# Attention on pairs of heads on partition halves, with the probabilities turned by a product with a diagonal and the output made with channels on partitions

## The chip, the cores and the metric

The kernel runs on one core of a Trainium2 chip (trn2), all in f32. The time is the device time of one execution in microseconds. A core has TensorE (PE; its weight loads are shown apart as PEld), VectorE (DVE), ScalarE (ACT), GpSimd (POOL) and SyncE (SP), which issues most DMAs.

## The reference, cut to what matters

Two blocks of two layers each follow one another on 256 tokens of width 1024 (the first block also on 256 context tokens). Three of the four mixers hold a softmax attention with heads of 64 channels; four query heads share a key head:

```python
def _softmax_attend(q, k, v):            # first block, layer 0
    s = jnp.einsum('bhgqd,bhkd->bhgqk', q, k, ...) * (ATT_HEAD_DIM ** -0.5)
    p = jax.nn.softmax(s, axis=-1).astype(v.dtype)
    return jnp.einsum('bhgqk,bhkd->bhgqd', p, v)
```

- First block, layer 0: 8 query heads, 2 key heads. The 256 context tokens see 256 keys, the 256 others see all 512. Its output is joined with that of a gated linear attention (GLA) and multiplied by `even_w_out`.
- Second block, layer 0: 16 query heads, 4 key heads, causal over 256 tokens.
- Second block, layer 1: the same heads, a causal window of 128 tokens, and a learned sink for each head: the maximum is taken over the logits and the sink, and exp(sink - m) is added to the sum.

Behind each of the two comes the product with `w_o`, a layer norm and a feed-forward part or a mixture of experts.

## The kernel before, in words

Tokens stand in tiles of 128 on the partitions; `hT` holds activations turned, channels on partitions, as the stationary operand of the next product. A stage is a function that adds a body for every engine; engines wait for one another by counted semaphores, and each stage ends with `meet()` (line 197), at which the four compute engines wait for one another. Within a stage each engine does its work in the order in which it is written. SyncE streams weights into a ring of three slots ahead of the stage that uses them.

`attend` (line 1034) is called three times: from `first_layer_even` (line 1569, two heads to a unit) and from `second_attention` (line 2451, four heads to a unit). For each key head `kv`:

- GpSimd copies the four query heads of the group into `att_qs` (line 1070), TensorE turns them, each 64 channels wide (line 1121), ScalarE and VectorE copy two heads each into the lower half of `hT` (lines 1165 and 1212). The keys of all key heads have been turned before (line 1079) and copied by ScalarE (line 1138). All turned queries and keys lie on partitions 0 to 63.
- The units of the key head run over tiles of queries and groups of heads: scores (line 1090, 64 rows of the array), on VectorE the mask where there is one (line 1182) and the maximum (lines 1187, 1191), on ScalarE the exponentials with their sums (line 1150), on TensorE the turning of the probabilities with `nc.tensor.transpose` (line 1101), ScalarE's copy of them (line 1160), then the output with the turned probabilities as weights and 64 columns of values moving (line 1110). VectorE divides by the sums as it takes the output, and writes it over the queries in `A` (lines 1203, 1205).
- TensorE's order is scores of unit i, turning of i-1, output of i-2 (lines 1126 to 1132), and it starts anew for each key head: the next queries are turned when all exponentials of the last head are done (line 1118).

The first attention has 16 units (8 with 256 keys, 8 with 512), each of the others 8 units of four heads (4 with 128 keys, 4 with 256).

`turn` (line 244) then turns the outputs with transposes, eight to a tile of tokens (line 256), ScalarE copies them into `hT` (line 263), and `project` (line 470) multiplies (line 504). In the first layer `gla_pairs` (line 791) stands between `attend` and `turn`; it has products on halves of the array's rows (line 854: two heads, partitions 0 to 63 and 64 to 127) and of its columns (line 872).

The expert products use column halves with `tile_position=(0, 64 * j)` (line 2673).

## Time and profile before

| | us |
|---|---|
| median of 3 runs | 3667.36 (3664.38 to 3670.75) |
| profiled execution | 3668.35 |
| its span | 3666.5 |
| mean granted clock of TensorE | 0.917 |

The page calls a stretch of time by its start and end from the span's start. In a timeline row stand the start, the length, the engine and line, the operation, what it writes and reads, its shape and how often it came; "weights rows*columns, then partitions x moving columns" is the shape of a matmul. A matmul of f32 operands appears as two instructions (passes), a transpose as one. The length of a row that joins several matmuls ends with a modelled end of the last; starts are measured. The clock column is the clock granted to TensorE as a share of 2.4 GHz.

### The profile page before, as it was taken

Reading aid. Unit: us, or ns where it says so; the run is one execution under the profiler, and the core shown is the slowest. Engines: PE = TensorE matmul, PEld = TensorE weight load, DVE = VectorE, ACT = ScalarE, POOL = GpSimd, SP = SyncE. Lnnn points to the kernel's source line nnn. Section 1 sums busy time; section 2 is a strip of 40 time slices with the busy share of each in tenths; the row PEclk is TensorE's granted clock in tenths of the full one; section 3 lists DMA queues with packets and bytes.
Section 4 is the critical chain, followed back from the end, with each engine's and each line's share of the span. In section 5 each row is a group of like instructions: output and inputs, shape, how many; then the busy total and the mean of one; then the engine's idle time right before and its main releaser. Section 6 shows DMA issues by size and latency. Waiting matters only on the chain.

```text
span 3666.5 us, 41927 instructions
## 1 busy us (share of the span) xinstructions
PE 3318.7 (91%) x18452; PEld 1955.5 (53%) x18452; DVE 819.8 (22%) x1241; ACT 452.6 (12%) x992; POOL 290.7 (8%) x286
## 2 busy tenths in 40 slices
PE   6959869999998999889988999977799999999996
PEld 2436644444447778756746677555344444434443
DVE  1032671000026656610012100223200000000002
ACT  1013212000012222210012000012000000000001
POOL 1010540000001222310000000000000000000000
PEclk9975878999999999989985999976799999999998
DMA  8750001120212121214330443130798999899982
GB/s 325 263 200 1 1 1 58 69 87 34 103 29 66 47 58 41 92 64 174 133 143 12 172 161 121 58 118 12 278 359 345 373 367 350 345 384 358 347 346 87
DMA packets 204261, 603.00 MB, mean 164 GB/s; under 512 B 5709, under 2 KB 46893, under 8 KB 197425
## 3 DMA queue, kind: packets, MB, share of 16 engines
q1 hardware_dynamic: 199664, 589.45, 42.4%
q0 software_dynamic: 3952, 10.26, 0.9%
q8 instruction: 149, 2.44, 0.3%
q10 hardware_dynamic: 464, 0.60, 0.1%
q14 instruction: 32, 0.25, 0.0%
HBM read 599.24 MB, written 1.05 MB: 164 GB/s over the span
## 4 chain that ended last, share of the span: by engine, by line
PE 85%; DVE 7%; issue 3%; ACT 2%; DMA 2%; POOL 1%; PEld 0%; POOLq 0%; PEldq 0%; ACTq 0%; DVEq 0%; SPq 0%
PE ps_ffn_gate L582 9%; PE ps_ffn_up L582 9%; PE ps_ffn_down L618 9%; PE ps_hg_step L1769 6%; PE ps_moe_down L2718 5%; PE ps_moe_gate L2673 5%; PE ps_moe_up L2673 5%; PE ps_project L504 4%; PE ps_lin L1432 3%; PE ps_moe_gate L2678 3%; PE ps_moe_up L2678 3%; PE ps_moe_down L2724 3%; PE ps_lin L296 2%; PE ps_att_s L1090 2%; PE ps_att_o L1110 2%
## 5 line engine op out<-in xcount | busy, mean ns | idle before, releaser
L582 PE MATMUL ps_ffn_gate<-hT,ring_buf 128*128 128x256 f32 (+1 forms) x1152 | 344.2, 453 | 6.4 <-DVEq L204 4.0
L582 PE MATMUL ps_ffn_up<-hT,ring_buf 128*128 128x256 f32 (+1 forms) x1152 | 336.7, 445 | 1.3
L618 PE MATMUL ps_ffn_down<-ring_buf,ffn_hiddenT 128*128 128x512 f32 x752 | 325.9, 593 | 3.0 <-issue 3.0
L582 PEld LDWEIGHTS ps_ffn_gate<-hT,ring_buf 128*128 128x128 f32 x1152 | 222.5, 194 | 122.6 <-issue 100.9
L582 PEld LDWEIGHTS ps_ffn_up<-hT,ring_buf 128*128 128x128 f32 x1152 | 217.9, 190 | 110.3 <-issue 90.0
L1769 PE MATMUL ps_hg_step<-ring_buf,hT 128*128 128x256 f32 (+1 forms) x1280 | 247.3, 353 | 18.6 <-ACT hg_kT L1872 16.2
L618 PEld LDWEIGHTS ps_ffn_down<-ring_buf,ffn_hiddenT 128*128 128x128 f32 x752 | 141.7, 190 | 182.0 <-issue 181.9
L1769 PEld LDWEIGHTS ps_hg_step<-ring_buf,hT 128*128 128x128 f32 x1280 | 215.0, 204 | 40.3 <-ACT hg_kT L1872 18.3
L662 DVE TENSOR_TENSOR ffn_hiddenT<-ffn_silu_buf,ps_ffn_up 128x256 f32<-128x256 f32 (+1 forms) x72 | 36.2, 502 | 757.8 <-PE ps_ffn_up L582 757.8
L2673 PE MATMUL ps_moe_up<-ring_buf,moe_xg_buf 128*64 128x512 f32 (+1 forms) x1024 | 199.5, 542 | 0.0
L2841 DVE TENSOR_TENSOR moe_hidden_buf<-moe_silu_buf,ps_moe_up 128x768 f32<-128x768 f32 (+1 forms) x32 | 27.3, 854 | 662.8 <-PE ps_moe_up L2678 590.3
L2718 PE MATMUL ps_moe_down<-ring_buf,moe_hiddenT 128*64 128x512 f32 x768 | 170.1, 595 | 0.0
L504 PE MATMUL ps_project<-ring_buf,hT 128*128 128x512 f32 x320 | 145.0, 615 | 2.7 <-ACTq L204 2.7
L2673 PE MATMUL ps_moe_gate<-moe_third,moe_xg_buf 128*64 128x512 f32 (+1 forms) x768 | 142.8, 524 | 0.0
L637 ACT ACTIVATE ffn_silu_buf<-ps_ffn_gate 128x256 f32<-128x256 f32 (+1 forms) x72 | 32.3, 449 | 849.7 <-PE ps_ffn_gate L582 849.7
L1432 PE MATMUL ps_lin<-ring_buf,hT 128*128 128x448 f32 (+1 forms) x384 | 134.1, 503 | 0.0
L2673 PEld LDWEIGHTS ps_moe_up<-ring_buf,moe_xg_buf 128*64 128x64 f32 x1024 | 70.7, 137 | 114.1 <-issue 106.0
L2783 ACT ACTIVATE moe_silu_buf<-ps_moe_gate 128x768 f32<-128x768 f32 (+1 forms) x32 | 23.4, 732 | 726.3 <-PE ps_moe_gate L2678 726.3
L2718 PEld LDWEIGHTS ps_moe_down<-ring_buf,moe_hiddenT 128*64 128x64 f32 x768 | 53.0, 137 | 104.0 <-issue 104.0
L1432 PEld LDWEIGHTS ps_lin<-ring_buf,hT 128*128 128x128 f32 x384 | 72.1, 193 | 66.5 <-issue 62.1
L504 PEld LDWEIGHTS ps_project<-ring_buf,hT 128*128 128x128 f32 x320 | 62.6, 198 | 83.2 <-issue 83.2
L2678 PE MATMUL ps_moe_up<-ring_buf,moe_xg_buf 128*32 128x256 f32 (+1 forms) x2048 | 103.5, 354 | 0.0
(456 smaller groups left out, 3721.0 us busy)
## 6 DMA issues: line engine op xcount, KB each, us to landing
...
moe_third<-in_w_exp_gate_dram SPq DMA_DIRECT2D x8, 2048.0 KB, 10.1
...
```

What stands on the lines that cost most here:

```text
L296: mm = nc.tensor.matmul(ps[n % 4][:, 0:hi - lo], hT[:, k, t * P:(t + 1) * P], view[:, k, o:o + hi - lo], start=k == 0, stop=k == parts - 1)
L504: mm = nc.tensor.matmul(ps_y[i % 2][:, h * 512:(h + 1) * 512], hT[:, k, t * P:(t + 1) * P], view[:, k, :], start=k == 0, stop=k == KD - 1)
L582: mm = nc.tensor.matmul(ps[:, 0:wide], view[:, k, i * P:(i + 1) * P], hT[:, k, first_col:first_col + wide], start=k == 0, stop=k == KD - 1)
L618: mm = nc.tensor.matmul(ps_y[i % 2][:, h, :], hidT[:, b, i * P:(i + 1) * P], view[:, b, h * 512:(h + 1) * 512], start=first, stop=end)
L1090: mm = nc.tensor.matmul(ps_s[i % 2][:, h, 0:nk], qT[:, g + h, qi * P:(qi + 1) * P], kT[:, bass.ds(kv, 1), 0:nk].rearrange("k h n -> k (h n)"),
L1110: mm = nc.tensor.matmul(ps_o[i % 2][:, h * E:(h + 1) * E], probsT[:, i % 2, h, k, :], A[:, t0 + k, bass.ds(kv * E + v_col, E)], start=k == ...
L1432: mm = nc.tensor.matmul(ps_lin[:, n % 4, 0:hi - lo], hT[:, k, t * P:(t + 1) * P], view[:, k, o:o + hi - lo], start=k == 0, stop=k == KD - 1)
L1769: mm = nc.tensor.matmul(ps[:, 0:width], hT[:, k, t * P:(t + 1) * P], view[:, k, 0:width], start=k == 0, stop=k == KD - 1)
L2673: nc.tensor.matmul(ps[j * 64:(j + 1) * 64, 0:half], xg[:, k, 0:WIDE], w[:, k, j * half:(j + 1) * half], start=k == 0, stop=k == KD - 1, ti ...
L2678: mm = nc.tensor.matmul(ps[j * 32:(j + 1) * 32, half:half + quarter], xg[:, k, WIDE:ROOM], w[:, k, j * quarter:(j + 1) * quarter], start=k ...
L2718: nc.tensor.matmul(ps_y[j * 64:(j + 1) * 64, 0:512], x, w[:, b, j * 512:(j + 1) * 512], start=c == 0 and b == 0, stop=c == NP - 1 and b == ...
L2724: mm = nc.tensor.matmul(ps_y[j * 32:(j + 1) * 32, 512:768], x, w[:, b, j * 256:(j + 1) * 256], start=c == 0 and b == 0, stop=c == NP - 1 a ...
```

## The change

(The lines that the diff removes from `attend` are those printed above; below stand the lines that it adds.)

The unit is now a pair of heads, 16 for each of the three calls, in one sequence over all key heads. A pair's turned queries lie on all 128 partitions, head 0 on 0 to 63 and head 1 on 64 to 127; the turned keys stand twice, once on each half, made by a product with the identity on the two column halves of the array. The score products of the two heads so lie on the two row halves. The queries and keys of the next key head are turned between the units of the last one, through one more PSUM bank; GpSimd has no part any more.

VectorE makes, from the sums, the inverse and two diagonal matrices (the identity scaled by the inverse of each row's sum). The probabilities are turned by a product with the diagonal, which divides as well; ScalarE copies head 0 of the result and VectorE head 1. In the output product the values are the weights (64 columns) and the turned probabilities move (128 columns), the two heads on the two column halves: the output comes with channels on partitions. ScalarE copies it to where the next projection reads it: over the queries in `A` in the first layer (where `project` now takes an accessor `of`), into `hT` in the second block. So `turn` handles four blocks instead of eight in the first layer and is gone from the second block. TensorE's order is scores of i, turning of i-2, output of i-3.

```diff
--- before.py
+++ after.py
-    def project(w, tiles, Y, seam):
+    def project(w, tiles, Y, seam, of=lambda k, t: hT[:, k, t * P:(t + 1) * P]):
...
-                            mm = nc.tensor.matmul(ps_y[i % 2][:, h * 512:(h + 1) * 512], hT[:, k, t * P:(t + 1) * P],
-                                                  view[:, k, :], start=k == 0, stop=k == KD - 1)
+                            mm = nc.tensor.matmul(ps_y[i % 2][:, h * 512:(h + 1) * 512], of(k, t), view[:, k, :],
+                                                  start=k == 0, stop=k == KD - 1)
...
+    def attend(A, q_col, k_col, v_col, kv_heads, q_tiles, room_T, made, mask=None, sinks=None, scale=1.0):
+        E = ATT_D
+        t0, nt = q_tiles[0][0], len(q_tiles)
         nkt = max(k for _, ks in q_tiles for k in ks) + 1 - t0
+        units = [(kv, qi, p) for kv in range(kv_heads) for qi in range(nt) for p in range(2)]
+        n, per = len(units), 2 * nt
+        step = 512 // (nt * P)
+        turns = [("k", 0)] + [("q", b) for b in range(0, 2, step)]
+        rounds = [(kv, kind, b) for kv in range(kv_heads) for kind, b in turns]
+        stands = {i: [] for i in range(n)}
+        for r, (kv, kind, b) in enumerate(rounds):
+            stands[0 if kv == 0 else (kv - 1) * per + 1 + r % len(turns)].append(r)
+        taken = lambda kind, r: sum(1 for x in rounds[:r + 1] if x[1] == kind)
+        ready_of = {"q": "att_q_ready", "k": "att_k_ready"}
+        keys_of = lambda u: q_tiles[units[u][1]][1]
         with ExitStack() as cx:
+            qT = hT[:, 0:4, :].rearrange("p k n -> p (k n)").rearrange("p (b n) -> p b n", n=nt * P) if nt == 4 else \
+                hT[:, :, 0:nt * P]
+            kT = sb(cx, "att_kT", [P, kv_heads, nkt * P])
+            probs = sb(cx, "att_probs_buf", [P, 2, 2, nkt * P])
+            diag = sb(cx, "att_diag_buf", [P, 2, 2, P])
+            masked = sb(cx, "att_masked", [P, 2, 2, nkt * P]) if mask is not None else None
+            stat = sb(cx, "att_stat", [P, 4, 4, 2])
+            probsT = room_T(cx, nkt)
+            ps_s = [pb(cx, f"ps_att_s{i}", [P, 2, 512]) for i in range(2)]
+            ps_t = pb(cx, "ps_att_t", [P, 2, 4, P])
+            ps_o = pb(cx, "ps_att_o", [P, 512])
+            ps_q = pb(cx, "ps_att_q", [P, 512])
             S = s_att
...
+                def stage(r):
+                    kv, kind, b = rounds[r]
+                    if r > 0:
+                        before = ready_of[rounds[r - 1][1]]
+                        pe.wait_ge(S[before].handle, S[before].at(taken(rounds[r - 1][1], r - 1)))
+                    if kind == "k":
+                        for i in range(nkt):
+                            for h in range(2):
+                                mm = nc.tensor.matmul(ps_q[h * E:(h + 1) * E, i * P:(i + 1) * P],
+                                                      A[:, t0 + i, k_col + kv * E:k_col + (kv + 1) * E], ident,
+                                                      start=True, stop=True, tile_position=(0, h * E))
+                    else:
+                        for x in range(step):
+                            for i in range(nt):
+                                at = q_col + (2 * kv + b + x) * 2 * E
+                                mm = nc.tensor.transpose(ps_q[:, (x * nt + i) * P:(x * nt + i + 1) * P],
+                                                         A[:, t0 + i, at:at + 2 * E], ident)
+                    mm.then_inc(S["att_staged"].handle, 1)
+                def scores(u):
+                    kv, qi, p = units[u]
+                    nk = len(keys_of(u)) * P
+                    r = max(x for x in range(len(rounds)) if rounds[x][0] == kv)
+                    pe.wait_ge(S["att_q_ready"].handle, S["att_q_ready"].at(taken("q", r)))
+                    pe.wait_ge(S["att_k_ready"].handle, S["att_k_ready"].at(taken("k", r)))
+                    pe.wait_ge(S["att_probs"].handle, S["att_probs"].at(u - 1))
+                    for h in range(2):
+                        mm = nc.tensor.matmul(ps_s[u % 2][:, h, 0:nk], qT[h * E:(h + 1) * E, 2 * kv + p, qi * P:(qi + 1) * P],
+                                              kT[h * E:(h + 1) * E, kv, 0:nk], start=True, stop=True)
+                def turned(u):
+                    pe.wait_ge(S["att_probs"].handle, S["att_probs"].at(u + 1))
+                    pe.wait_ge(S["att_diag"].handle, S["att_diag"].at(u + 1))
+                    pe.wait_ge(S["att_T_ready_a"].handle, S["att_T_ready_a"].at(u))
+                    pe.wait_ge(S["att_T_ready_v"].handle, S["att_T_ready_v"].at(u))
+                    for h in range(2):
+                        for k in range(len(keys_of(u))):
+                            mm = nc.tensor.matmul(ps_t[:, h, k, :], probs[:, u % 2, h, k * P:(k + 1) * P], diag[:, u % 2, h, :],
+                                                  start=True, stop=True)
+                def output(u):
+                    kv, qi, p = units[u]
+                    keys = keys_of(u)
+                    pe.wait_ge(S["att_T_ready_a"].handle, S["att_T_ready_a"].at(u + 1))
+                    pe.wait_ge(S["att_T_ready_v"].handle, S["att_T_ready_v"].at(u + 1))
+                    pe.wait_ge(S["att_taken"].handle, S["att_taken"].at(u))
+                    for k in range(len(keys)):
+                        for h in range(2):
+                            mm = nc.tensor.matmul(ps_o[h * E:(h + 1) * E, 0:P], A[:, t0 + k, v_col + kv * E:v_col + (kv + 1) * E],
+                                                  probsT[:, u % 2, h, k, :], start=k == 0, stop=k == len(keys) - 1,
+                                                  tile_position=(0, h * E))
...
+                for i in range(n + 3):
+                    if i < n:
+                        for r in stands[i]:
+                            stage(r)
+                        scores(i)
+                    if 2 <= i < n + 2:
+                        turned(i - 2)
+                    if i >= 3:
+                        output(i - 3)
...
+                def queries(r):
+                    kv, kind, b = rounds[r]
+                    act.wait_ge(S["att_staged"].handle, S["att_staged"].at(r + 1))
+                    nc.scalar.activation(qT[:, 2 * kv + b:2 * kv + b + step, :],
+                                         ps_q[:, :].rearrange("p (x n) -> p x n", x=step), ACT.Copy, scale=scale)\
+                        .then_inc(S["att_q_ready"].handle, 1)
+                def softmax(u):
+                    nk = len(keys_of(u)) * P
+                    act.wait_ge(S["att_max"].handle, S["att_max"].at(u + 1))
+                    act.wait_ge(S["att_turned"].handle, S["att_turned"].at(u - 1))
+                    src = ps_s[u % 2] if mask is None else masked[:, u % 2, :, :]
+                        nc.scalar.activation(stat[:, u % 4, 3, :], stat[:, u % 4, 3, :], ACT.Exp)
+                    for h in range(2):
+                        last = nc.scalar.activation(probs[:, u % 2, h, 0:nk], src[:, h, 0:nk], ACT.Exp,
+                                                    bias=stat[:, u % 4, 0, h:h + 1], accum_out=stat[:, u % 4, 1, h:h + 1])
+                def take_turned(u):
+                    nk = len(keys_of(u))
+                    act.wait_ge(S["att_turned"].handle, S["att_turned"].at(u + 1))
+                    act.wait_ge(S["att_out"].handle, S["att_out"].at(u - 1))
+                    nc.scalar.activation(probsT[:, u % 2, 0, 0:nk, :], ps_t[:, 0, 0:nk, :], ACT.Copy)\
+                        .then_inc(S["att_T_ready_a"].handle, 1)
+                def take(u):
+                    kv, qi, p = units[u]
+                    act.wait_ge(S["att_out"].handle, S["att_out"].at(u + 1))
+                    nc.scalar.activation(made(2 * kv + p, qi), ps_o[:, 0:P], ACT.Copy).then_inc(S["att_taken"].handle, 1)
+                for i in range(n + 3):
+                    if i < n:
+                        for r in stands[i]:
+                            if rounds[r][1] == "q":
+                                queries(r)
+                    if 2 <= i < n + 2:
+                        take_turned(i - 2)
+                    if i < n:
+                        softmax(i)
+                    if i >= 3:
+                        take(i - 3)
...
+                def keys(r):
+                    kv, kind, b = rounds[r]
+                    dve.wait_ge(S["att_staged"].handle, S["att_staged"].at(r + 1))
+                    nc.vector.tensor_copy(kT[:, kv, :], ps_q[:, 0:nkt * P]).then_inc(S["att_k_ready"].handle, 1)
+                def maxima(u):
+                    kv, qi, p = units[u]
+                    nk = len(keys_of(u)) * P
+                    dve.wait_ge(S["att_scores"].handle, S["att_scores"].at(u + 1))
+                    src = ps_s[u % 2][:, :, 0:nk]
+                    top = stat[:, u % 4, 0, :]
+                        link_v(nc.vector.tensor_tensor(masked[:, u % 2, :, 0:nk], src,
+                                                       mask[:, qi, 0:nk].unsqueeze(1).to_broadcast([P, 2, nk]), ALU.add))
+                        src = masked[:, u % 2, :, 0:nk]
+                        nc.vector.tensor_reduce(top, src, AX.X, ALU.max, negate=True).then_inc(S["att_max"].handle, 1)
+                        own = sinks[:, 4 * kv + 2 * p:4 * kv + 2 * p + 2]
+                        nc.vector.tensor_tensor(stat[:, u % 4, 3, :], top, own, ALU.add)\
+                def take_turned(u):
+                    nk = len(keys_of(u))
+                    dve.wait_ge(S["att_turned"].handle, S["att_turned"].at(u + 1))
+                    dve.wait_ge(S["att_out"].handle, S["att_out"].at(u - 1))
+                    nc.vector.tensor_copy(probsT[:, u % 2, 1, 0:nk, :], ps_t[:, 1, 0:nk, :])\
+                        .then_inc(S["att_T_ready_v"].handle, 1)
+                def diagonal(u):
+                    total, inverse = stat[:, u % 4, 1, :], stat[:, u % 4, 2, :]
+                    dve.wait_ge(S["att_probs"].handle, S["att_probs"].at(u + 1))
+                        link_v(nc.vector.tensor_tensor(total, total, stat[:, u % 4, 3, :], ALU.add))
+                    for h in range(2):
+                        last = nc.vector.tensor_scalar(diag[:, u % 2, h, :], ident, stat[:, u % 4, 2, h:h + 1], None, ALU.mult)
+                    last.then_inc(S["att_diag"].handle, 1)
+                for i in range(n + 2):
+                    if i < n:
+                        for r in stands[i]:
+                            if rounds[r][1] == "k":
+                                keys(r)
+                        maxima(i)
+                    if i >= 2:
+                        take_turned(i - 2)
+                    if i < n:
+                        diagonal(i)
+            for k in ("att_scores", "att_max", "att_probs", "att_diag", "att_turned", "att_T_ready_a", "att_T_ready_v",
+                      "att_out", "att_taken"):
...
+        attended = lambda b, t: A[:, t, O_AQ + b * P:O_AQ + (b + 1) * P]
         silu_columns(A, O_G, O_Z)
         gla_gates(A, g, T, lambda: even_queries_keys(A))
-        attend(A, O_AQ, O_AK, O_AV, 2, [(0, (0, 1)), (1, (0, 1)), (2, (0, 1, 2, 3)), (3, (0, 1, 2, 3))], 2)
+        attend(A, O_AQ, O_AK, O_AV, 2, [(0, (0, 1)), (1, (0, 1)), (2, (0, 1, 2, 3)), (3, (0, 1, 2, 3))],
+               lambda cx, nkt: hT[:, 4:8, :].rearrange("p k n -> p (k n)")
+               .rearrange("p (b h t n) -> p b h t n", b=2, h=2, t=nkt), attended)
         gla_pairs(A, g, T)
-        turn(lambda t, k: A[:, t, O_G + k * P:O_G + (k + 1) * P] if k < 4 else
-             A[:, t, O_AQ + (k - 4) * P:O_AQ + (k - 3) * P], ALL_TILES)
+        turn(lambda t, k: A[:, t, O_G + k * P:O_G + (k + 1) * P], ALL_TILES, 4)
 
...
             rotate_partly(B, rot)
-            attend(B, 0, K2, V2, 4, [(0, (0,)), (1, (0, 1))], 4, mask=mask, sinks=sinks, scale=ATT_D ** -0.5)
-            turn(lambda t, k: B[:, t - 2, k * P:(k + 1) * P], LAT_TILES)
+            attend(B, 0, K2, V2, 4, [(0, (0,)), (1, (0, 1))],
+                   lambda cx, nkt: sb(cx, "att_probsT", [P, 2, 2, nkt, P]),
+                   lambda b, qi: hT[:, b, (2 + qi) * P:(3 + qi) * P], mask=mask, sinks=sinks, scale=ATT_D ** -0.5)
 
...
         with ExitStack() as cy:
-            project(a["even_w_out"][0], ALL_TILES, A[:, :, 0:D], GatedSeam(cy, 0, 0, (0, 1), ALL_TILES))
+            project(a["even_w_out"][0], ALL_TILES, A[:, :, 0:D], GatedSeam(cy, 0, 0, (0, 1), ALL_TILES),
+                    lambda k, t: hT[:, k, t * P:(t + 1) * P] if k < 4 else
+                    A[:, t, O_AQ + (k - 4) * P:O_AQ + (k - 3) * P])
```

## Rows read from the trace of the kernel before

**Rows 1.** The page, part 1: busy time, share, instructions

```profile
PE 3318.7 (91%) x18452; PEld 1955.5 (53%) x18452; DVE 819.8 (22%) x1241; ACT 452.6 (12%) x992; POOL 290.7 (8%) x286
```

**Rows 2.** Stretches: us, busy of PE, PEld, DVE, ACT, POOL, clock, DMA share, GB/s

```profile
275.35:389.47 114.12, 107.89 (x393) 79.35 (x393) 25.07 (x50) 34.42 (x84) 2.07 (x2) 0.56 0.00 1
1909.68:1992.13 82.45, 63.07 (x249) 52.63 (x249) 22.84 (x36) 26.53 (x81) 2.45 (x4) 0.50 0.08 30
1992.13:1997.16 5.03, 3.68 (x17) 3.28 (x17) 0.00 (x0) 2.05 (x2) 0.00 (x0) 0.50 0.00 0
2442.44:2527.86 85.42, 63.36 (x249) 52.64 (x249) 28.08 (x68) 27.30 (x89) 2.46 (x4) 0.50 0.00 0
2527.86:2532.52 4.66, 3.31 (x16) 3.07 (x16) 0.00 (x0) 2.05 (x2) 0.00 (x0) 0.70 0.00 0
```

**Rows 3.** Timeline, one unit of the first attention: start, us, instruction, times

```profile
309.68 3.78 PE L1090 MATMUL ps_att_s<-att_kT,hT 64*128 64x512 f32 x4
...
313.39 1.97 PE L1101 MATMUL ps_att_t<-const,att_probs_buf 128*128 128x128 f32 x8
313.49 1.22 DVE L1187 TENSOR_REDUCE att_stat<-ps_att_s 128x2 f32<-128x1024 f32 x1 [3.22 <-PE ps_att_s L1090]
...
315.15 3.52 PE L1110 MATMUL ps_att_o<-even_A,hT 128*128 128x64 f32 x16
...
316.31 0.68 ACT L1150 ACTIVATE att_probs_buf<-ps_att_s,att_stat 128x512 f32<-128x512 f32 x1
...
317.54 0.21 ACT L1150 ACTIVATION_READ_ACCUMULATOR att_probs_buf<-ps_att_s,att_stat 128x1 f32 x1
...
318.59 3.78 PE L1090 MATMUL ps_att_s<-att_kT,hT 64*128 64x512 f32 x4
```

**Rows 4.** Stretches around changes of the clock, columns as in rows 2

```profile
325.60:329.00 3.40, 3.40 (x18) 3.40 (x18) 0.46 (x2) 1.07 (x4) 0.00 (x0) 0.50 0.02 5
329.00:330.00 1.00, 1.00 (x11) 1.00 (x10) 0.00 (x0) 0.72 (x1) 0.00 (x0) 0.97 0.00 0
381.50:388.50 7.00, 7.00 (x34) 6.88 (x32) 0.46 (x2) 1.02 (x1) 0.00 (x0) 0.50 0.00 0
2527.86:2530.60 2.74, 2.74 (x13) 2.74 (x14) 0.00 (x0) 0.74 (x1) 0.00 (x0) 0.50 0.00 0
2531.00:2532.00 1.00, 0.17 (x2) 0.00 (x0) 0.00 (x0) 0.79 (x1) 0.00 (x0) 1.00 0.00 0
```

**Rows 5.** Timeline: weight loads of 512-column passes at the low clock

```profile
1999.03 0.34 PEld L504 LDWEIGHTS ps_project<-ring_buf,hT 128*128 128x128 f32 x1 [0.52 <-issue]
1999.88 0.34 PEld L504 LDWEIGHTS ps_project<-ring_buf,hT 128*128 128x128 f32 x1 [0.52 <-issue]
```

**Rows 6.** Groups by form on TensorE: busy us, mean ns, idle before

```profile
L2673 PE MATMUL ps_moe_up<-ring_buf,moe_xg_buf 128*64 128x512 f32 x768 | 170.1, 595 | 0.0
...
L1798 PE MATMUL ps_rec_scores<-ring_buf 128*128 128x128 f32 x448 | 57.1, 280 | 2.1 <-DVE ring_buf L2007 1.8 <-DVE ring_buf L1995 0.3
```

**Rows 7.** Timeline behind the first attention: products on halves of the array

```profile
407.04 1.83 PE L854 MATMUL ps_pair_scores<-hT,pair_kd 64*128 64x128 f32 x28 [0.41 <-DVE ring_buf L971]
...
408.67 0.42 PE L857 MATMUL ps_pair_scores<-pair_qT,pair_kT 64*128 64x128 f32 x4
...
411.39 0.71 PE L868 MATMUL ps_pair_out<-even_A,hT 128*128 128x128 f32 x4 [0.16 <-DVE hT L978]
...
412.03 0.44 PE L872 MATMUL ps_pair_out<-even_A,hT 128*64 128x128 f32 x4
```

**Rows 8.** Timeline of the second attention, a unit of 128 keys

```profile
1976.05 0.69 DVE L1182 TENSOR_TENSOR att_masked<-ps_att_s,att_mask 128x512 f32<-128x512 f32 x1 [2.18 <-PE ps_att_s L1090]
...
1977.50 0.40 ACT L1150 ACTIVATE att_probs_buf<-att_masked,att_stat 128x128 f32<-128x128 f32 x1 [3.72 <-DVE att_stat L1187]
...
1978.19 0.19 ACT L1150 ACTIVATION_READ_ACCUMULATOR att_probs_buf<-att_masked,att_stat 128x1 f32 x1
```

**Rows 9.** Groups by form on VectorE: a scaling by a column

```profile
L2824 DVE TENSOR_SCALAR moe_pick_buf<-const,moe_place 128x96 f32<-128x96 f32 x18 | 4.1, 265 | 2.0 <-issue 2.0
```

153 lines of the change are left out of this document (6 added, 147 removed).

## The prediction

> **What bounds the kernel now.** I read the page's engine shares first: TensorE is busy 91% of the span [rows 1]. A share does not say what a stage waits for, so I cut out the stretches that the change touches [rows 2]: the first layer's attention, 114.12 us, the two attentions of the second block, 82.45 and 85.42 us, and the turning behind each, 5.03 and 4.66 us. Together 292 us, 8% of the span. In the first TensorE is busy 107.89 of 114.12 us, in the others 63 of 82 and 63 of 85; no other engine reaches half, and the DMA engines rest. The reader should see the clock column: 0.50 to 0.56 of full speed, the lower of the two levels (1.2 of 2.4 GHz), while dense products elsewhere run at 1.00.
>
> One unit of the first attention (two heads, 512 keys) shows TensorE as the bound: scores at 309.68, turning 313.39, output 315.15, next scores 318.59, so 8.91 us without a hole [rows 3]. An f32 product is two passes in the trace, a transpose one. At the low clock a 512-column pass takes 0.85 us [rows 5]: four make 3.41, leaving 0.30 us between the scores (64 rows of the array) and the turning (128 rows). Turning: 8 passes, 1.76 us, 0.22 each. Output: 16 passes of 64 columns, 0.215 each, what 128 columns cost: the 128-column weights set it, so the array streams half of the time.
>
> **Why the clock is low** decides this case. It rose behind 325.60 to 329.00 (outputs, then a full turning): 0.50 there, 0.97 in the microsecond after. It rose behind 2527.86 to 2530.60, nothing but transposes: 1.00 from 2531. It did not rise in 381.50 to 388.50, 7 us with TensorE busy throughout, on 64-column outputs alone [rows 4], nor in the sixteen units with their scores on half the rows [rows 2, 3]. So every rise had a run of work on 128 rows and 128 columns ahead of it, and the scores and 64-column outputs brought none. In the new kernel the score products use both row halves, the turning is 128 columns on 128 rows and twice as long, and the outputs move 128 columns on both column halves: a unit is almost all such work. I take it that the first attention runs mostly at 2.4 GHz.
> The Trainium skill (TensorE: Matmul & The Clock Gate, Part 4) says that the full clock does not set in for transposes in transpose mode. The rise at 2530 disagrees [rows 4]. By that rule the replaced transposes alone would explain the low clock, and all three attentions would be fast: the all-fast case below, whose time I work out from rows.
>
> **The change, part by part.** Prices per pass: 128 columns 0.215 us at the low clock [rows 3] and 57.1/448 = 0.127 at the high one; 512 columns 0.85 and 0.43. Column halves side by side: 170.1/768 = 0.22 for a 512-column pass, half of 0.43 [rows 6]. Row halves side by side: 28 passes from 407.04 to 408.67, 0.058 each against 0.107 (a quarter of 0.43) alone [rows 7]. A pair of score products has only four passes; the two of one head cannot overlap each other, so I count three slots of four. A change of array shape costs 0.30 low [rows 3]; high, the full products at 411.39 need 4 x 0.107 = 0.43, their successors on column halves start at 412.03, so 0.21 [rows 7]. The new unit has three changes where the old had one. The old one from output to scores shows no hole; I take 0.5 (high) and 0.7 (low) per unit, bounds 0.2 and 1.2.
> TensorE per unit at the high clock: 256 keys: scores 3 x 0.21, turning 8 x 0.127 (two passes now, not one), output 8 x 0.064, changes 0.5: 2.67 us. 512 keys: 1.29 + 2.03 + 1.02 + 0.5 = 4.84. At the low clock: 4.57 and 8.42; 128 keys 2.7.
> The chain over VectorE and ScalarE is new: maxima, exponentials, diagonal, then the next maxima, since the diagonal of a unit stands ahead of them on VectorE. Maximum 1.22 us for 1024 elements [rows 3], 0.69 for 512 (as the masking [rows 8]), so 0.42 for 256. Exponentials of two heads: 0.88 us at 128 keys [rows 8], 1.44 at 512 [rows 3], 1.07 between. Reciprocal 0.2, two scalings of a 128-wide identity 0.54 (nearest row 0.265 for 96 wide [rows 9]; bounds 0.17 and 0.40 each). Hand-overs 0.15. That is 2.6 and 3.55 us in the first attention, just under TensorE's high-clock figures, so TensorE still binds there. The copies of the turned block run on both engines inside TensorE's time.
> First attention: 8 x 2.67 + 8 x 4.84 = 60.1; start at the low clock, in series through one bank: keys 16 passes on column halves 1.7, VectorE's copy 0.7, two groups of four transposes 0.86 and their copies of 512 columns 0.6 (as the f32 exponential of 512 takes 0.68 [rows 3]), five hand-overs of 0.15 to 0.2: 6.2; second key head's staging 2.5; clock rising late 3; fill and last units 4. Sum 76, saved 38. GpSimd's copies and the stop for each key head are gone, the K staging is dearer (products on column halves) and inside the 6.2.
> Second attention: unmasked chain plus the masking: 128 keys 0.88 + 0.88 + 0.74 + 0.15 = 2.65, 256 keys 3.4. A key head (two of each, 0.4 for keys) is 12.5 us on that chain; on TensorE at the low clock 16.6 with 2.1 of staging. The high clock leaves TensorE resting about half of the 128-key units, so I expect both levels in turn and take the middle, 14.6; ends 12.5 and 16.6. Times 4, plus 9.2 (an estimate: a start half as long as the first's, 3.3, as it has half the key tiles and one query group; 5.9 for ScalarE's table, fill and last units, bounds 3 and 8): 67.6, saved 14.9. The turning behind it goes: 5.0.
> Third: the sinks add four short VectorE steps and an exponential of 2 columns, 0.9 us per unit: 16.1 by the chain, 17.1 by TensorE, middle 16.6; times 4 plus 10.1 = 76.5, saved 8.9; its turning 4.7.
> The first layer's turning loses 16 of 32 transposes, 3.4. The stages behind start at the higher clock: 16 transposes after the first attention at 0.11 less each, 1.7, and 1 in the projection after the second. The weights of these stages had landed before the attention ended and do not take back the gain: the DMA share is 0.00 to 0.08 there [rows 2].
> Sum: 38 + 14.9 + 5.0 + 8.9 + 4.7 + 3.4 + 2.7 = 77.6 us. The profiled execution took 3668.35 us (span 3666.5, 1.85 around it), 1.0 above the median 3667.36: 3590.7 against it, **3590** against the median.
>
> **The rivals.**
> All fast: the clock holds in all three, the chain alone binds: 23.2 + 10.9 instead of 14.9 + 8.9, 1 more behind: 3578.
> Clock stays low: the holes at shape changes and the waits for the diagonal keep it down, as in [rows 2]. Turning doubles (+1.7 us per 512-key unit), outputs halve (-1.7), scores lose a quarter: the first attention is 117.8 us, 3.7 worse; the others save 6.8 and 6.9 by keeping the queue filled, plus 13.1 of turning: 3644. For it: 16 old units in a row failed to lift the clock; against it: what failed to lift it is gone.
> The halves do not overlap for so few passes: 17 us in the first attention, 10 in the others: 3617. Against it [rows 6, 7].
> Slower: the shape changes. Place: three per unit, 48 units, all on TensorE; price: I count 0.23 us each at the low clock. The low-clock case has 23 us in hand, so it decides from 0.16 us more for each; at 0.5 in all, 144 x 0.27 = 39 us more: 3683. Against it: the one hole seen is 0.30, and one of the three shows none.
> The Trainium skill (TensorEngine Tiling (Array Packing), Key Properties) says that a change of tiling mode drains the TensorE, without a price; both holes [rows 3, 7] agree, and it speaks for this rival.
> No change: the whole gain falls where others wait. Nothing else runs in these stretches, so I give it little.
>
> **How the numbers follow.** Forecast case 0.50, all fast 0.22, halves not overlapping 0.08, low clock 0.13, slower 0.04, no change 0.03. A measurement of this kernel tells about 0.2% (7 us) from no change. Faster 0.93, same 0.03, slower 0.04. Range: below, all fast less 14 us for cheaper scalings and shape changes, 3564; above, past 3617 and short of the low-clock case, 3636: this leaves out the cases at 3644 and above, 0.20.
>
> **What would show it.** The first attention at a clock above 0.8, about 76 us, its 512-key unit near 4.8 us with TensorE dense; the product turning x192 passes in the first layer instead of 96; the second and third attention near 68 and 77 us with VectorE's maxima starting right behind its diagonals; no turning behind them, 16 transposes in the first layer's. Wrong if the clock column still says 0.5 in the first attention, or if the score-to-turning hole has grown.

## The result, and the profile after

The changed kernel takes 3561.26 us, median of four executions (3559.05 to 3565.35), beside 3668.13 for the kernel before on the same chip: ratio 0.9711, 95% interval 0.9694 to 0.9728, so 107 us less. I had forecast 3590, 78 less, with a range from 3564 up. The direction and the places were right; the gain is more than a third larger, and the time is 3 us below the range. The profiled executions, 3668.35 and 3565.35 us, differ by 103.0; the sums below are made on these two.

The page after, parts 1 and 2 (compare [rows 1]):

```profile
span 3563.5 us, 42668 instructions
...
PE 3231.7 (91%) x18620; PEld 1874.9 (53%) x18620; DVE 850.4 (24%) x1433; ACT 445.0 (12%) x1052; POOL 285.7 (8%) x276
...
PEclk9978979999999999989998999887999999999998
```

TensorE's share is 91% as before: nothing on this line says where 103 us went. The stretches do (columns as in [rows 2]): the first, second and third attention, the second and third now up to the projection, as no turning stands between; then the first attention cut in two:

```profile
274.98:340.29 65.31, 61.80 (x497) 45.18 (x497) 33.80 (x82) 31.86 (x100) 0.00 (x0) 0.88 0.01 1
1857.44:1914.01 56.57, 43.24 (x305) 30.76 (x305) 32.62 (x100) 26.56 (x101) 0.00 (x0) 0.80 0.11 45
2359.82:2429.70 69.88, 51.42 (x305) 36.98 (x305) 43.13 (x164) 28.33 (x117) 0.00 (x0) 0.66 0.00 1
...
274.98:290.00 15.02, 12.75 (x65) 8.87 (x66) 4.57 (x11) 3.72 (x11) 0.00 (x0) 0.50 0.00 0
290.00:340.29 50.29, 49.05 (x434) 36.31 (x432) 29.23 (x71) 28.14 (x89) 0.00 (x0) 0.99 0.01 2
```

Read the clock column first. The first attention starts at the lower level (1.2 GHz) and from 290 on has 0.99, the upper one, with TensorE busy 49.05 of 50.29 us. The later two are another kind of stage: TensorE rests 13 and 18 us in them, VectorE has 33 and 43, and the clock goes up and down (0.80, 0.66).

Where the 103.0 us lie, from the starts of the stages in the two traces:

| stretch | before | after | saved | forecast |
|---|---|---|---|---|
| first attention | 114.12 | 65.31 | 48.8 | 38 |
| GLA behind it | 153.10 | 146.97 | 6.1 | 1.7 |
| first turning | 7.52 | 4.70 | 2.8 | 3.4 |
| second attention and turning | 87.48 | 56.57 | 30.9 | 19.9 |
| third attention and turning | 90.08 | 69.88 | 20.2 | 13.6 |
| recurrent stage and all up to the second attention | 806.31 | 812.47 | -6.2 | 0 |
| all the rest | | | 0.3 | 1 |

The three attentions with their turnings gave 99.9 us (forecast 71.5). GLA's further 6.1 and the recurrent stage's -6.2 cancel but for 0.1. Neither stage's code was touched. In GLA TensorE is busy 99.62 us instead of 105.72, at a clock of 0.87 instead of 0.82; in the recurrent stage the same 512 passes of one form take longer. Groups by form on TensorE, before:

```profile
L1769 PE MATMUL ps_hg_step<-ring_buf,hT 128*128 128x128 f32 x512 | 73.2, 308 | 16.2 <-ACT hg_kT L1872 16.2
```

and after:

```profile
L1786 PE MATMUL ps_hg_step<-ring_buf,hT 128*128 128x128 f32 x512 | 76.1, 316 | 16.2 <-ACT hg_kT L1889 16.2
```

The mean clock of the whole stretch is 0.95 instead of 0.96. Cut into slices of 4.25 us, both traces have the dips of the clock at nearly the same places of the stage; in some the low level lasts longer after. I read this as the stage starting at another moment; no run tests it. Over the runs below this stretch took 806, 809 to 810, or 812 to 813 us, in no order that follows the attention's forms (before 806, old_forms 809, after 812).

Two rounds of TensorE's order in the first attention, 512 keys, timeline of its matmuls after, the clock high (compare [rows 3]):

```profile
324.14 1.13 PE L1096 MATMUL ps_att_s<-att_kT,hT 64*128 64x512 f32 x4
325.20 2.05 PE L1107 MATMUL ps_att_t<-att_diag_buf,att_probs_buf 128*128 128x128 f32 x16
327.18 0.66 PE L1119 MATMUL ps_att_o<-hT,even_A 128*64 128x128 f32 x8
327.77 1.13 PE L1096 MATMUL ps_att_s<-att_kT,hT 64*128 64x512 f32 x4
328.83 2.05 PE L1107 MATMUL ps_att_t<-att_diag_buf,att_probs_buf 128*128 128x128 f32 x16
330.81 1.09 PE L1119 MATMUL ps_att_o<-hT,even_A 128*64 128x128 f32 x16
```

Start to start: four score passes of 512 columns 1.06 us, two times 0.43 and 0.20 for the change of shape, so **two slots, where I counted three**. Sixteen turning passes 1.98, output 1.09 for sixteen passes on column halves. A 512-key unit is about 4.1 us; I had 4.84. At 0.107 us for each 128 columns [rows 7] the turning holds 0.27 us and the output 0.23 us beyond their passes, besides the 0.20 behind the scores.

VectorE's own timeline in the second attention after, a unit of 256 keys:

```profile
1878.22 0.68 DVE L1193 TENSOR_TENSOR att_masked<-ps_att_s,att_mask 128x512 f32<-128x512 f32 x1
1878.94 0.69 DVE L1197 TENSOR_REDUCE att_stat<-att_masked 128x2 f32<-128x512 f32 x1
1879.55 0.28 DVE L1210 COPY att_probsT<-ps_att_t 128x128 f32<-128x128 f32 x1
1880.79 0.17 DVE L1218 RECIPROCAL att_stat<-att_stat 128x2 f32<-128x2 f32 x1 [0.96 <-ACT att_probs_buf L1151]
1880.99 0.48 DVE L1220 TENSOR_SCALAR att_diag_buf<-const,att_stat 128x128 f32<-128x128 f32 x2
1881.38 0.68 DVE L1193 TENSOR_TENSOR att_masked<-ps_att_s,att_mask 128x512 f32<-128x512 f32 x1
```

This is the forecast chain: the reciprocal waits 0.96 us for the exponentials, the next masking starts as the diagonals end, 3.16 us from unit to unit (3.4 forecast), though TensorE had begun the next scores at 1878.50. A key head is 11.5 us (its staging starts at 1861.40, 1872.97 and 1884.46).

### The profile page after: what moved, and what is told of

It reads as the page before. It is cut to its first block, busy times and chain, and to the rows that moved or that the text cites. A ratio compares the mean times of both kernels' runs of the same rounds, so it can differ in the third digit from the quotient of the medians.

```text
span 3563.5 us, 42668 instructions
## 1 busy us (share of the span) xinstructions
PE 3231.7 (91%) x18620; PEld 1874.9 (53%) x18620; DVE 850.4 (24%) x1433; ACT 445.0 (12%) x1052; POOL 285.7 (8%) x276
## 4 chain that ended last, share of the span: by engine, by line
PE 82%; DVE 9%; issue 3%; ACT 2%; DMA 2%; POOL 1%; PEld 0%; POOLq 0%; PEldq 0%; ACTq 0%; DVEq 0%; SPq 0%
PE ps_ffn_gate L582 9%; PE ps_ffn_up L582 9%; PE ps_ffn_down L618 9%; PE ps_hg_step L1786 7%; PE ps_moe_down L2736 6%; PE ps_moe_gate L2691 6%; PE ps_moe_up L2691 6%; PE ps_project L504 4%; PE ps_lin L1447 4%; PE ps_moe_up L2696 3%; PE ps_moe_gate L2696 3%; PE ps_moe_down L2742 3%; PE ps_lin L296 2%; PE ps_rec_sums L1796 1%; PE ps_rec_scores L1815 1%
## 5 line engine op out<-in xcount | busy, mean ns | idle before, releaser
L2691 PEld LDWEIGHTS ps_moe_up<-ring_buf,moe_xg_buf 128*64 128x64 f32 x1024 | 70.7, 137 | 114.1 <-issue 106.0
L504 PE MATMUL ps_project<-ring_buf,hT 128*128 128x512 f32 x256 | 119.2, 624 | 1.4 <-ACTq L204 1.4
L2801 ACT ACTIVATE moe_silu_buf<-ps_moe_gate 128x768 f32<-128x768 f32 (+1 forms) x32 | 23.4, 730 | 726.4 <-PE ps_moe_gate L2696 726.4
L1447 PEld LDWEIGHTS ps_lin<-ring_buf,hT 128*128 128x128 f32 x384 | 71.8, 192 | 66.7 <-issue 62.3
L296 PE MATMUL ps_lin<-ring_buf,hT 128*128 128x384 f32 x256 | 88.4, 509 | 9.1 <-DMA ring_buf<-in_w_qkv_dram 7.4
```

The costliest lines, as they stand in the source:

```text
L296: mm = nc.tensor.matmul(ps[n % 4][:, 0:hi - lo], hT[:, k, t * P:(t + 1) * P], view[:, k, o:o + hi - lo], start=k == 0, stop=k == parts - 1)
L504: mm = nc.tensor.matmul(ps_y[i % 2][:, h * 512:(h + 1) * 512], of(k, t), view[:, k, :], start=k == 0, stop=k == KD - 1)
L1447: mm = nc.tensor.matmul(ps_lin[:, n % 4, 0:hi - lo], hT[:, k, t * P:(t + 1) * P], view[:, k, o:o + hi - lo], start=k == 0, stop=k == KD - 1)
L2691: nc.tensor.matmul(ps[j * 64:(j + 1) * 64, 0:half], xg[:, k, 0:WIDE], w[:, k, j * half:(j + 1) * half], start=k == 0, stop=k == KD - 1, ti ...
```

## Experiments

Each is one edit of the changed kernel, unless it says otherwise. I compare stretches: runs that leave out the division or a head's result hand on other values, and the part behind the third attention, with the mixture of experts, then takes another time: 1284 us in turn_transpose and 1411 us in unpaired_transpose, 1134 in the changed kernel. Whole, these two took 3701.24 and 3857.42 us, longer than the kernel before, and say nothing of the attentions. The table has us and mean clock of the three attentions in one profiled execution of each, without the turning that stands behind the second and third in before and before_product. Only before, after, dve_order and order_scalar_takes were executed more than once. old_output, old_forms, old_forms_stop and stop_heads_early ran on another chip, on which the kernel before took 3672.30 us, beside 3667.6 for the other runs below; 5 us in the whole is the measure for differences between the two groups.

| kernel | 1st, clock | 2nd, clock | 3rd, clock |
|---|---|---|---|
| before | 114.1, 0.56 | 82.4, 0.50 | 85.4, 0.50 |
| after | 65.3, 0.88 | 56.6, 0.80 | 69.9, 0.66 |
| same_rows | 76.7, 0.88 | 60.5, 0.75 | 74.2, 0.57 |
| wide_output | 71.5, 0.92 | 55.6, 0.88 | 71.0, 0.69 |
| old_output | 70.6, 0.92 | 58.4, 0.77 | 71.4, 0.57 |
| turn_transpose | 59.1, 0.90 | 54.9, 0.66 | 69.0, 0.57 |
| unpaired_transpose | 75.0, 0.85 | 62.5, 0.70 | 73.0, 0.61 |
| old_forms | 93.7, 0.66 | 69.8, 0.50 | 74.2, 0.50 |
| old_forms_stop | 111.9, 0.58 | 86.5, 0.50 | 100.6, 0.50 |
| stop_heads | 71.8, 0.90 | 80.0, 0.63 | 91.6, 0.63 |
| stop_heads_early | 67.7, 0.92 | 73.8, 0.68 | 86.8, 0.61 |
| dve_order | 63.4, 0.90 | 47.7, 0.86 | 62.2, 0.68 |
| order_scalar_takes | 62.9, 0.91 | 44.0, 0.92 | 52.6, 0.88 |
| before_product | 115.0, 0.67 | 74.6, 0.73 | 83.0, 0.61 |

In the first attention the mean clock is mostly the moment of one rise. In every run without stops TensorE has 0.50 from the start, then 1.00 to the end: the rise comes 16.0 us behind the start in after, 19.0 in same_rows, 11.8 in wide_output, 11.4 in old_output, 11.2 in turn_transpose, 22.4 in unpaired_transpose and 63.6 in old_forms. Each moment is read from one execution.

### What the forms are worth

**same_rows**: the second head's scores on the first head's row half.

```diff
-                        mm = nc.tensor.matmul(ps_s[u % 2][:, h, 0:nk], qT[h * E:(h + 1) * E, 2 * kv + p, qi * P:(qi + 1) * P],
-                                              kT[h * E:(h + 1) * E, kv, 0:nk], start=True, stop=True)
+                        mm = nc.tensor.matmul(ps_s[u % 2][:, h, 0:nk], qT[0:E, 2 * kv + p, qi * P:(qi + 1) * P],
+                                              kT[0:E, kv, 0:nk], start=True, stop=True)
```

> The changed kernel with the second head's score product put on the same row half as the first (it reads the first head's queries and keys, so its scores are those of the first head). Theory 'two slots': the four passes of a pair stand beside one another two by two, so this adds two passes to each score pair: 2 x 0.43 = 0.86 us for 512 keys and 0.43 us for 256 keys at the high clock, 8 units of each in the first attention = 10.3 us, which goes from 65.3 to about 76 us; in the later two, whose pace VectorE and ScalarE set, 1 to 4 us each. Rival 'no overlap' (the short scores came from the clock alone): nothing is added, 65 us stays. Rival 'three slots' (as I forecast): half, about 70 us.

Whole run 3583.26 us. The first attention rose by 11.4 us (10.3 expected) at the same clock:

```profile
275.64:352.37 76.73, 73.48 (x496) 52.17 (x497) 35.09 (x82) 31.20 (x100) 0.00 (x0) 0.88 0.00 1
```

Its timeline at the high clock has 1.91 us from scores to turning, where the changed kernel has 1.06:

```profile
327.54 1.98 PE L1096 MATMUL ps_att_s<-att_kT,hT 64*128 64x512 f32 x4
329.45 1.16 PE L1107 MATMUL ps_att_t<-att_diag_buf,att_probs_buf 128*128 128x128 f32 x8
```

That is 2 x 0.43 more: the passes of a pair stand fully beside one another. The slot that I counted too many is half of this, 8 x (0.43 + 0.21) = 5.1 us; the rest of the 11.4 us goes with the rise of the clock, 3 us later. In the later two it adds 3.9 and 4.3 us (1 to 4 expected); their clock fell too, to 0.75 and 0.57.

**wide_output**: outputs with 128 columns of values as weights, one head behind the other.

```diff
-                    for k in range(len(keys)):
-                        for h in range(2):
-                            mm = nc.tensor.matmul(ps_o[h * E:(h + 1) * E, 0:P], A[:, t0 + k, v_col + kv * E:v_col + (kv + 1) * E],
+                    wide = v_col + min(kv, kv_heads - 2) * E
+                    for h in range(2):
+                        for k in range(len(keys)):
+                            mm = nc.tensor.matmul(ps_o[:, h * P:(h + 1) * P], A[:, t0 + k, wide:wide + 2 * E],
```

> The changed kernel with the output products not on column halves: the weights are the values of two key heads (128 columns), and the second head's product goes behind the first's, to other columns of the bank (its result is not used, and all 128 channels of the pair are the first head's). Theory 'column halves overlap fully': the slots double, 8 x 0.107 = 0.86 us more for 512 keys and 0.43 us for 256, 8 units of each = 10.3 us: first attention 65.3 to 76 us at the same clock; later two 0 to 4 us more. Rival 'column halves do not overlap' : nothing is added.

3571.92 us. The first attention took 71.5 us, 6.2 more, at a higher clock (0.92); TensorE's busy time rose by 6.4. Its timeline at the high clock:

```profile
326.88 1.16 PE L1107 MATMUL ps_att_t<-att_diag_buf,att_probs_buf 128*128 128x128 f32 x8
327.87 1.06 PE L1120 MATMUL ps_att_o<-hT,even_A 128*128 128x128 f32 x8
328.86 1.13 PE L1096 MATMUL ps_att_s<-att_kT,hT 64*128 64x512 f32 x4
```

The output of a 256-key unit takes 0.99 us from start to start, against 0.59 on column halves, so the overlap is real. The turning ahead of it takes 0.99 instead of 1.08, so about 0.1 us of each unit was the change to column halves; and the clock rose 4.2 us earlier, which at half the time for each pass is some 2 us. Together they account for most of what lacks to the 10.3 expected. The second attention did not take longer at all, its clock being 0.88.

**old_output**: turned probabilities as weights, 64 columns of values moving.

```diff
-                            mm = nc.tensor.matmul(ps_o[h * E:(h + 1) * E, 0:P], A[:, t0 + k, v_col + kv * E:v_col + (kv + 1) * E],
-                                                  probsT[:, u % 2, h, k, :], start=k == 0, stop=k == len(keys) - 1,
-                                                  tile_position=(0, h * E))
+                            mm = nc.tensor.matmul(ps_o[:, h * E:(h + 1) * E], probsT[:, u % 2, h, k, :],
+                                                  A[:, t0 + k, v_col + kv * E:v_col + (kv + 1) * E],
+                                                  start=k == 0, stop=k == len(keys) - 1)
```

> The changed kernel with the output products in the form of the kernel before: the turned probabilities as weights (128 columns), 64 columns of values moving, 192 passes in the first attention that don't share slots (the result then stands with queries on partitions, where channels are awaited). Theory 'the old output form costs its passes alone': 192 passes x 0.107 to 0.127 us against 96 slots: 65.3 + 8 to 12 = 73 to 77 us at a granted clock over 0.85. Rival 'this form holds the clock down': clock 0.50 to 0.65 and over 90 us.

3576.36 us; 70.6 us at 0.92. Beside the other new forms the old output costs 5.3 us in the first attention (8 to 12 expected; the clock rose 4.6 us earlier), and it does not hold the clock down there. In the third the clock is 0.57 instead of 0.66.

**turn_transpose**: `nc.tensor.transpose(..., ident)` in place of the product with the diagonal, which is still made.

> The changed kernel with the probabilities turned by the transpose (one pass) in place of the product with the diagonal of inverse sums (two passes); the diagonals are still made, but the division is left out of the result. Theory 'the clock comes from dense work, whatever the form of the turning': the granted clock of the first attention stays near 0.88 and its 96 turnings save one pass each, 96 x 0.107 to 0.127 = 10 to 12 us, to about 54 us; in the later attentions under 2 us each. Rival 'the product feeds the clock': the granted clock falls to 0.50 to 0.60 and the first attention takes 75 to 95 us, longer than the 65.3 us with the product.

The clock stayed high (0.90): the rival falls. The size missed. TensorE's busy time fell by 12.6 us, as reckoned, and the stage by 6.2: 

```profile
276.31:335.37 59.06, 49.18 (x400) 31.52 (x400) 33.25 (x82) 32.14 (x100) 0.00 (x0) 0.90 0.00 1
```

TensorE now rests 9.9 us, against 3.5: its turnings wait eight times, 4.1 us in all, for VectorE's copy of the block before, so with one pass less TensorE is no longer the only bound. In the later attentions the transposes bring 1.7 and 0.9 us; their clock fell to 0.66 and 0.57, and TensorE's busy time in the second stayed at 43.2 us with 48 passes fewer.

**before_product**, an edit of the kernel before: its transposes of probabilities are products with the identity.

```diff
-                            mm = nc.tensor.transpose(ps_t[:, h, k, :], probs[:, i % 2, h, k * P:(k + 1) * P], ident)
+                            mm = nc.tensor.matmul(ps_t[:, h, k, :], probs[:, i % 2, h, k * P:(k + 1) * P], ident,
+                                                 start=True, stop=True)
```

> The kernel before with one edit: the 96 + 48 + 48 transposes of the probabilities are products with the identity, two passes for one. Theory 'this alone does not lift the clock': first attention 114 us + 96 x 0.215 = 135 us at a granted clock of 0.56, second and third + 48 x 0.215 = 10 us each. Rival 'the product feeds the clock': the granted clock of the first attention goes above 0.8 and the stage falls below 100 us although it has more passes.

3656.79 us: 192 passes more, and the run is 11 us shorter than its neighbour of 3667.6. That neighbour's seven executions go down to 3655.35, so the total alone would not carry it. The mean clock of the whole run does, 0.932 against 0.916 to 0.921 in those seven, and so do the stretches:

```profile
275.86:390.90 115.04, 108.22 (x489) 82.85 (x489) 25.08 (x50) 34.37 (x84) 2.07 (x2) 0.67 0.00 1
1907.62:1982.23 74.61, 54.80 (x296) 48.28 (x297) 22.84 (x36) 26.09 (x81) 2.45 (x4) 0.73 0.08 33
```

The first attention stayed at 115 us, its added passes paid by a clock of 0.67; the second lost 7.8 us, 0.73 instead of 0.50. Neither theory had this: with the second pass the clock was higher in all three attentions, but not 0.8.

### Order and stops

**unpaired_transpose**: the edits of same_rows, wide_output and turn_transpose together.

> The three edits together: both heads' scores on one row half, outputs not on column halves, transposes in place of the products with diagonals (the division is left out, and results of the second head are not used). TensorE's forms are then those of the kernel before, with the changed kernel's order and no stop between key heads. Theory 'a dense order alone lifts the clock': first attention at a clock of 0.85 to 0.95, 59.1 (with transposes alone) + 11.4 + 10.3 = 81 us. Rival 'the forms set the clock' (pairs and products): the clock falls to 0.50 to 0.65 and the stage goes over 100 us, near the 114 us of before. Second attention: clock 0.50 to 0.60, 58 to 70 us.

75.0 us at 0.85, so the rival of over 100 us falls; the second attention took 62.5 us as expected, but at 0.70. The forms are not all those of before, as I had written: the output still has 128 columns of values as weights. **old_forms** also puts the old output form in, so all forms of TensorE in the units are the old ones.

> All four of TensorE's forms of before (scores of both heads on one row half, transposes in place of products, turned probabilities as weights of the output) in the changed kernel's order, without stops between key heads (the division is left out, and the result does not stand where it is awaited). Theory 'order and density set the clock, not the forms': near the run with unpaired forms and wide outputs, 72 to 80 us at 0.80 to 0.90 in the first attention, 58 to 66 us in the second. Rival 'the old output form is what keeps the clock low': over 95 us at 0.50 to 0.65.

3632.77 us; 93.7 us at 0.66 in the first attention, between the theories, and 0.50 throughout the other two. The clock did rise in the first attention, 63.6 us behind its start, and then held for 30 us to its end, with all the old forms:

```profile
277.26:340.80 63.54, 61.37 (x210) 43.29 (x210) 20.54 (x48) 18.48 (x58) 0.00 (x0) 0.50 0.00 1
341.00:370.98 29.98, 28.91 (x191) 22.52 (x190) 14.26 (x34) 13.55 (x42) 0.00 (x0) 1.00 0.00 1
```

The kernel before, besides a short one near 282, has such a rise too, 53.7 us behind its start, but loses it again in the first units behind the stop between its two key heads:

```profile
275.35:329.00 53.65, 50.64 (x168) 35.72 (x169) 11.62 (x21) 16.77 (x42) 2.07 (x2) 0.53 0.00 1
329.10:339.60 10.50, 8.17 (x62) 7.18 (x62) 3.52 (x7) 3.16 (x7) 0.00 (x0) 0.99 0.00 0
339.70:389.47 49.77, 48.88 (x165) 36.25 (x164) 9.93 (x22) 14.38 (x36) 0.00 (x0) 0.50 0.00 0
```

**old_forms_stop** adds the stop between key heads: PE, ACT and DVE run their loops once for each key head, and the next keys and queries are turned behind the last output.

```diff
-            stands[0 if kv == 0 else (kv - 1) * per + 1 + r % len(turns)].append(r)
+            stands[kv * per].append(r)
...
-                for i in range(n + 3):
-                    if i < n:
+                for i, j in ((kv * per + j, j) for kv in range(kv_heads) for j in range(per + 3)):
+                    if j < per:
```

> The same old forms, and the stop between key heads put back. What is left of the change is the distance of two units between scores and turning, the two PSUM tiles for turned values and the order of the engines. Theory 'the stops lower the clock, and that is most of what before lost': first attention 80 to 95 us, second and third 80 to 92 us at a clock of 0.50 to 0.65. Rival 'something else in the old order (turning one unit behind the scores) costs the most': not over 80 us in the first.

3689.52 us. The first attention is 111.9 us at 0.58, near the 114.1 at 0.56 of before, and its clock goes as there: up 53.9 us behind the start, down behind the stop. I expected 80 to 95, and the rival not over 80: both missed. The later two came out at 86.5 and 100.6 us (80 to 92 expected). Before has 82.4 and 85.4 us there, so this is not the kernel before: it turns keys and queries in series at each stop, and has twice as many units of half the size. What the 15 us more in the third attention consist of stays open. **stop_heads** has the same stop with the new forms.

> The changed kernel with the stop between key heads put back: every engine ends the units of one key head before the keys and queries of the next are turned (1 boundary in the first attention, 3 in each later one). Theory 'the running through is part of the gain': a boundary costs an emptying and a filling of the pipeline, 3 to 5 us: first attention 65.3 + 4 = 69 us, second 56.6 + 9 to 15, third 69.9 + 9 to 15 us, more where the clock falls in the stops. Rival 'the gain is the passes and the clock': under 1 us for a boundary, stages within 3 us of the changed kernel's.

3614.08 us. One boundary cost 6.5 us in the first attention, three cost 23.4 and 21.7 in the later two, above the upper ends of 5 and 15; the clock of the later two fell to 0.63, while in the first it stayed at 1.00 through the stop. TensorE at one boundary, timeline:

```profile
1879.99 0.67 PE L1119 MATMUL ps_att_o<-att_probsT,qkv 128*64 128x128 f32 x8 [0.47 <-ACT hT L1165]
1880.48 0.62 PE L1077 MATMUL ps_att_q<-const,qkv 128*64 128x128 f32 x8
1881.61 0.66 PE L1084 MATMUL ps_att_q<-const,qkv 128*128 128x128 f32 x4 [0.52 <-DVE att_kT L1184]
1882.95 0.71 PE L1096 MATMUL ps_att_s<-att_kT,hT 64*128 64x128 f32 x8 [0.69 <-ACT hT L1139]
1885.43 0.70 PE L1096 MATMUL ps_att_s<-att_kT,hT 64*128 64x256 f32 x4 [1.76 <-ACT att_probs_buf L1151]
```

**stop_heads_early** keeps the stop, but turns the next keys and queries during the units ahead (the `stands` line as in the changed kernel).

> The stop between key heads as in stop_heads (71.8, 80.0 and 91.6 us in the three attentions), but the keys and queries of the next key head are turned during the units of the one before, as in the changed kernel, so only the emptying and filling is left. Theory 'a boundary's 7 us is half staging in a row (turn keys, copy, turn queries, copy), half emptying and filling': 69, 68 to 72 and 79 to 83 us. Rival 'the emptying is all': within 2 us of stop_heads.

3597.18 us; 67.7, 73.8 and 86.8 us, outside the ranges of both theories. Staging in a row is 4.0 us of the first attention's boundary and 2.1 and 1.6 us of each later one; emptying and filling 2.4, 5.7 and 5.6. Staging and emptying both count; in the later attentions the emptying is most of it, and dearer than I expected.

The four corners, forms and stops crossed:

| | old forms, stops | old forms, none | new forms, stops | new forms, none |
|---|---|---|---|---|
| first | 111.9, 0.58 | 93.7, 0.66 | 71.8, 0.90 | 65.3, 0.88 |
| second | 86.5, 0.50 | 69.8, 0.50 | 80.0, 0.63 | 56.6, 0.80 |
| third | 100.6, 0.50 | 74.2, 0.50 | 91.6, 0.63 | 69.9, 0.66 |

In the first attention the forms, with the clock that they bring, are worth 28 to 40 us and the stop 6 to 18. In the other two it is the other way round: the stops of an attention 17 to 26 us, the forms 4 to 13.

### The chain

**dve_order**: VectorE makes the maxima of a unit ahead of the diagonals of the one before.

```diff
                         maxima(i)
+                    if 1 <= i <= n:
+                        diagonal(i - 1)
                     if i >= 2:
                         take_turned(i - 2)
-                    if i < n:
-                        diagonal(i)
```

> The changed kernel with VectorE's order changed: the maxima of a unit come ahead of the diagonals of the unit before it, so the chain maxima, exponentials, diagonals, next maxima is cut. Theory 'the chain bounds the second and third attention': each loses 5 to 12 us (from 56.6 and 69.9 us), the first (TensorE 62 of 65 us busy) at most 2 us; whole run 3562 -> 3540 to 3555 us. Rival 'TensorE and its clock bound them': under 2 us each, or a gain that a fallen clock gives back.

3545.86 us (3543.71 to 3546.23); to before 0.967, interval 0.9649 to 0.9691. The second attention lost 8.9 us, the third 7.7, the first 1.9, all within what the chain's theory had: in the later two the chain, and not TensorE alone, set the pace. **order_scalar_takes** also leaves both heads' copies of turned probabilities to ScalarE in the masked attentions.

```diff
-                    nc.scalar.activation(probsT[:, u % 2, 0, 0:nk, :], ps_t[:, 0, 0:nk, :], ACT.Copy)\
+                    nc.scalar.activation(probsT[:, u % 2, 0:both, 0:nk, :], ps_t[:, 0:both, 0:nk, :], ACT.Copy)\
...
-                    if i >= 2:
+                    if i >= 2 and both == 1:
                         take_turned(i - 2)
```

> The reordered kernel (VectorE makes the maxima of a unit ahead of the diagonals of the unit before), and in the masked attentions ScalarE copies the turned probabilities of both heads, so VectorE has 16 copies less of 0.28 to 0.42 us (5 us) and ScalarE's copies are longer by 16 x 0.2 = 3 us. Theory 'VectorE's copy behind two maxima still holds TensorE's next turning' (7 and 8 waits, 4.8 and 9.6 us, in the reordered run): second attention 47.7 -> 43 to 46, third 62.2 -> 55 to 60 us, run 3535 to 3543 us. Rival 'TensorE bounds them now': within 1 us of the reordered kernel.

3536.81 us (3529.56 to 3544.25); to before 0.9651, interval 0.9633 to 0.9669. Its slowest execution is below the changed kernel's fastest, 3559.05; against dve_order the intervals overlap. The later two attentions, in the profile of 3529.56 us:

```profile
1855.36:1899.33 43.97, 37.59 (x305) 26.66 (x305) 27.79 (x84) 29.10 (x101) 0.00 (x0) 0.92 0.14 55
2340.77:2393.40 52.63, 40.15 (x304) 28.53 (x304) 37.90 (x148) 30.67 (x117) 0.00 (x0) 0.88 0.00 1
```

They lost another 3.7 and 9.5 us, the third more than expected: the clock goes from 0.68 to 0.88, and TensorE's busy time falls from 50.0 to 40.2 us for the same passes. I read the clock as a consequence of TensorE running denser with the wait for VectorE's copy gone (9.6 us in dve_order). The profile is of the fastest of four executions; two others took 3542.67 and 3544.25 us, about as long as dve_order, and have no profile. By its median it is the fastest version of this study.

## Why the prediction was right and wrong

**The sum.** The profiled executions differ by 103.0 us, the forecast had 77.6. The three attentions with their turnings gave 28.4 more than forecast (10.8, 11.0 and 6.6), all other stretches together 3 less. The lower end of the range, 3564, was the all-fast case less 14, with the first attention still at 76.

**The clock.** Right for the first attention: above 0.8, after a start at the low level, with TensorE as the bound. The reading of [rows 4], that low clock went with scores on half the rows and outputs of 64 columns, holds in part only. It says that none of the sixteen old units lifted the clock, and [rows 4] itself has a rise at 329, in the middle of them; what was lost behind the stop was this rise. With the old output alone (old_output) or the old scores alone (same_rows) the clock is high all the same; with all old forms it is 0.66, 0.50, 0.50. No single form decides; in the first attention the forms went with the moment of the rise (16.0 us, or 63.6 with all old ones), and the stop in before and old_forms_stop with its loss. Why the rise comes at 22.4 us in unpaired_transpose and at 63.6 in old_forms, which differ in the output form alone, stays open; each is one execution. The rival that the clock stays low, given 0.13, is out.

**The page on transposes.** Products in place of transposes raised the clock in the kernel before (0.50 to 0.73 in the second attention), and transposes lowered it in the new (0.80 to 0.66). So the rule of the Trainium skill (TensorE: Matmul & The Clock Gate, Part 4) points the right way here, though not as an absolute: turn_transpose runs its first attention at 0.90, and old_forms, with every probability turned by a transpose, its last 30 us there at 1.00. I had set the rule aside for one rise.

**First attention, forecast 76, measured 65.3.** The failed step is the sum per unit, 2.67 and 4.84 us. "I count three slots of four": the runs show two, 0.43 us less for a 512-key unit and 5.1 of the 10.7 us missed. The high-clock price of 0.127 per 128-column pass was a mean over a stage that also holds waits and low clock; at 0.107 the 24 slots of turning and output are 0.48 less. The changes of shape are 0.70 instead of 0.5. That is 4.13 us, as measured. Eight such units and eight at 2.3 (256 keys: scores 0.63, turning 1.08, output 0.59 from start to start) make 9 us less; start, fill and late clock, reckoned as 16, were 14. That the outputs share slots on column halves was right.

**Second and third, forecast 67.6 and 76.5, measured 56.6 and 69.9.** The chain was found, and priced a little too dear; the failed step is "take the middle" between its pace and that of TensorE at the low clock. A key head took 11.5 us in the second, not 14.6, below the chain's own 12.5; about 15.5 in the third (stagings at 2364.00, 2379.90 and 2394.92) instead of 16.6, with its clock at 0.66. The rival "all fast" described the second attention better than my forecast.

**What the work between key heads costs** I had no term of its own for: it sat in the low-clock rival's "keeping the queue filled", 6.8 and 6.9 us for the later attentions. Stop and no stop at the same clock of 0.50 and the same forms differ by 16.7 and 26.4 us. That the new kernel can do without stops is the main part of its gain in these two stages: with stops it has 80.0 and 91.6 us against before's 87.5 and 90.1 with the turnings, so one stage 7.5 us faster and one 1.5 us slower. This stop is dearer than before's, which had turned its keys ahead; with the staging done early (stop_heads_early) they take 73.8 and 86.8 us.

**Shape changes.** Priced at 0.5 us per unit at the high clock. What a 512-key unit holds beyond its slots at 0.107 is 0.20 us behind the scores, 0.27 behind the turning and 0.23 behind the output, 0.70 in all; how much of the last two is the change itself is not separated, save the 0.1 of wide_output. The rival that they make the kernel slower is out. **Halves do not overlap** is out, by same_rows. **Stages behind**: 2.7 us forecast; GLA gave 6.1 and the recurrent stage took 6.2. **First turning**: 2.8 us instead of 3.4, its clock being 0.50 instead of 0.67.
